# Scratch memory laid out anew, and VectorE's row sums of the feed-forward moved ahead of weight lows

## The chip, the cores and the metric

One NeuronCore of a Trainium2 chip runs the whole program. The metric is the device time of one execution in microseconds (us). Engines are named as in the profile: PE is TensorE's matmuls and PEld its weight loads, DVE is VectorE, ACT ScalarE, POOL GpSimd, SP the engine that issues the loads from HBM.

## What is computed

Four transformer layers over 512 tokens of width 1024, in fp32: two layers of a first stack (differential attention beside a gated linear recurrence, then a feed-forward part and a gate), two of a second (pooling mixer beside sparse attention, then a feed-forward part). The change touches the feed-forward parts, whose hidden width is 4096:

```python
h = h + jnp.square(jax.nn.relu(hm @ w_mlp_in[l])) @ w_mlp_out[l]      # layers 0 and 1
f = jnp.square(jax.nn.relu(h @ w_ff1[l])) @ w_ff2[l]                  # layers 2 and 3
x = x + rms_norm_2(f, g_post_ffn[l])
```

## The kernel before

**Products.** Activations lie transposed, 128 features on the partitions and 512 tokens along them. A fp32 product is made of three reduced-precision passes: each operand is split in a high part (a rounded copy, made by ScalarE) and a low part (value minus high part, made by VectorE), and TensorE adds high·high, high·low and low·high (`three_passes`, L472). Weights come in chunks of 1 MB (128 x 2048 values) in two raw buffers `wr`; `split_high` (L406) writes `wh`, `split_low` (L412) writes `wl`. SP loads chunk c once the low of chunk c - 2 is made (`load_chunk`, L375), since the raw buffer is then free.

**The feed-forward part** is done in four blocks of 1024 hidden features. A block has four input chunks (c0 to c0 + 3; each gives two tiles of hidden features in PSUM) and four output chunks. The first three blocks of every layer, twelve in all, are "fast": their output products are done by a seven-product scheme for 2 x 2 blocks, which needs sums and differences of quarters of the hidden tiles and of the weights. Blocks are counted from j = 0.

**VectorE in a fast block** (`fast_block_dve`) has for each input chunk i = 0 to 3, with p counting the pairs of tiles:
- `rectify` (L703): drains the even tile from PSUM, times the root of the mean square `rb`;
- `even_low` (L809, L810): its low part (128 x 256), and a first difference of quarters;
- `rectify` of the odd tile;
- for i < 2 the `split_low` (L412) of input chunk c0 + i + 2, not in block 0 of layers 2 and 3, where it was made earlier; for i = 2 four `form_low` (L781, 128 x 512 each) for the first output chunk;
- `other_sums` (L818, L819, L821), three sums of 128 x 256;
- for i = 3 one more `form_low`;
- `odd_low` (L828), 128 x 512;
- `sums_low` (L835, L838): the low of the first difference, 128 x 256, and of the three sums, 128 x 768, which go to the tile `rounded`.

**ScalarE** (`fast_block_act`) squares each tile (L789, L790), copies the high of the first difference (L796) between the two tiles, then `split_high` or four `form_high` (L769), then the high of the three sums (L802), which waits for L821. It works in the order it is given, and so does every engine.

**GpSimd** (`fast_block_pool`) forms four sums of 128 x 512 of the raw quarters of each output chunk (`sum_weights`, L752, L754, L756, L757) as soon as it is loaded. The second output chunk's load waits for the low of input chunk c0 + 3. Between them `carry` (L945) adds partial results to the output rows.

**TensorE** goes through the four input chunks (24 matmuls a tile) and straight on to the first output chunk (`fast_products`). There its first product needs L809 of pair 3 after three of four parts, and the four next products take their last part at the end, which needs L838 of pair 3. A tile's bank is free after its `rectify`.

**Layers 2 and 3** add the output to rows `branch(k)` in the scratch tile `arena`, which GpSimd zeroes with two memsets (L2070) before the first fast block; VectorE waits for them (`zeroed`) ahead of its first `rectify`. The first addition to these rows is `add_quarter` (L937), after the first output products.

**Memory.** Each partition holds, in this order: `gh`, `gl`, `hh`, `hl` (16 KB each), `arena` (15376 values, with `rounded` laid over the same place), `x`, `wr`, `wh`, `wl` (16 KB each), then small tiles.

Of the kernel before, what the change touches and what calls it, by code (L numbers as in the profile page):

```python
# [29 lines left out]
F32R = mybir.dt.float32r  # L30
# [6 lines left out]
P = 128  # L37
D = 1024
S = 512
# [8 lines left out]
BC = D // CW  # L48
FAST = FB - 1
HALF = S // 2  # L50
PAIRS = KT // 2
# [87 lines left out]
def build(nc, weights, params_a, params_b, gains, gates, embed, constants, positions, xt, out):  # L139

    with ExitStack() as ctx:
        def sb(name, shape, dtype=F32):
            return ctx.enter_context(nc.sbuf_tensor(name, shape, dtype))


        tiles = {name: sb(name, [P, KT, S], F32R) for name in ("gh", "gl", "hh", "hl")}
        with nc.sbuf_tensor("rounded", [P, ARENA], F32R) as rounded:
            pass
        arena = sb("arena", [P, ARENA])
        rest = dict(  # L150
            x=sb("x", [P, KT, S]), wr=sb("wr", [P, 2, CHUNK]), wh=sb("wh", [P, 2, CHUNK], F32R), wl=sb("wl", [P, 2, CHUNK], F32R),
            cst=sb("cst", [P, C_N]), par=sb("par", [P, max(AP_N, BP_N)]), rb=sb("rb", [P, S]), sq=sb("sq", [P, 2, S]),
            tmp=sb("tmp", [P, 4, S]), small=sb("small", [P, 256]), extra=sb("extra", [P, 7 * HALF + 2 * S]), rounded=rounded, arena=arena,
            ps=ctx.enter_context(nc.psum_tensor("ps", [P, 8, S], F32)))
        memories = [Memory(tiles["gh"], tiles["gl"], tiles["hh"], tiles["hl"], **rest),
                    Memory(tiles["hh"], tiles["hl"], tiles["gh"], tiles["gl"], **rest)]

        sets = [semaphores(nc, ctx, f"set{n}_", SET) for n in range(2)]
        shared = dict(zip(SHARED.split(), semaphores(nc, ctx, "shared", len(SHARED.split()))))
        stages = []  # L160
        for n in range(2 * DEPTH):
            stages.append(Stage(n, stages[-1] if stages else None, memories[n % 2], sets[n % 2], shared))
        for stage, following in zip(stages, stages[1:]):
            stage.following = following
        programs = []
        for n, stage in enumerate(stages):
            if n < DEPTH:
                programs.append(first_stack_layer(stage, n, weights, params_a, gains, gates, embed, constants, xt,
                                                  positions[0:P, :], positions[P:2 * P, :]))
            else:  # L170
                programs.append(second_stack_layer(stage, n - DEPTH, weights, params_b, gains, positions[P:2 * P, :], out))

        with nc.Block() as block:
            @block.sync
            def _(sp):
                for program in programs:
                    program["sp"](sp)

            @block.gpsimd
            def _(pool):  # L180
                for program in programs:
                    program["pool"](pool)

            @block.scalar
            def _(act):
                for program in programs:
                    program["act"](act)

            @block.vector
            def _(dve):  # L190
                for program in programs:
                    program["dve"](dve)

            @block.tensor
            def _(pe):
                for program in programs:
                    program["pe"](pe)
        used = [sem.num for sem in sets[0] + sets[1] + list(shared.values())]
        clear(nc, range(min(used), max(used) + 1))
# [138 lines left out]
ARENA = 15376  # L338
# [361 lines left out]
def rectify(dve, mem, sem, tile, k, per=once, bank=None):  # L700

    dve.wait_ge(sem["product"], tile + 1 + per(4 * BC))
    dve.scalar_tensor_tensor(out=mem.tmp[:, k % 2, :], in0=mem.ps[:, tile % 4 if bank is None else bank, :], scalar=0.0, in1=mem.rb[:, :],  # L703
                             op0=ALU.max, op1=ALU.mult).then_inc(sem["drained"], 1)
# [123 lines left out]
    dve.tensor_tensor(mem.hl[:, k, :], mem.tmp[:, 3, :], mem.hh[:, k, :].bitcast(F32), ALU.subtract).then_inc(sem["hidden_low"], 1)  # L828


def sums_low(dve, mem, sem, p):

    q = p % PAIRS
    dve.wait_ge(sem["sums_high"], 2 * p + 1)
    dve.tensor_tensor(mem.hl[:, 2 * q, HALF:S], mem.tmp[:, 2, 0:HALF], mem.hh[:, 2 * q, HALF:S].bitcast(F32), ALU.subtract)  # L835
    dve.wait_ge(sem["sums_high"], 2 * p + 2)
    dve.wait_ge(sem["hidden_sums"], 4 * p + 3)
    dve.tensor_tensor(mem.tl[:, q, :], mem.sums, mem.th[:, q, :].bitcast(F32), ALU.subtract).then_inc(sem["hidden_sums"], 1)  # L838
# [133 lines left out]
def fast_block_dve(dve, mem, sem, c0, j, tile_of, split_ahead, bank, target):  # L972

    for i in range(BC):
        p = PAIRS * j + i
        rectify(dve, mem, sem, tile_of[c0 + i], 2 * i, bank=bank(tile_of[c0 + i]))
        even_low(dve, mem, sem, p)
        rectify(dve, mem, sem, tile_of[c0 + i] + 1, 2 * i + 1, bank=bank(tile_of[c0 + i] + 1))
        if i < 2 and split_ahead:
            split_low(dve, mem, sem, c0 + i + 2)  # L980
        if i == 2:
            form_low(dve, mem, sem, c0 + BC, range(4))
        other_sums(dve, mem, sem, p)
        if i == 3:
            form_low(dve, mem, sem, c0 + BC, (4,))
        odd_low(dve, mem, sem, p)
        sums_low(dve, mem, sem, p)
    for oc in range(BC):
        g, c = BC * j + oc, c0 + BC + oc
        rows = target(2 * oc), target(2 * oc + 1)  # L990
        ahead = oc + 1 < BC
        if oc == 0:
            form_low(dve, mem, sem, c, (5, 6))
        first_partial(dve, mem, sem, g)
        if oc:
            form_low(dve, mem, sem, c, (6,))
        add_quarter(dve, mem, sem, g, "t", 3, rows[0][:, HALF:S])
        add_quarter(dve, mem, sem, g, "v", 4, rows[1][:, HALF:S])
        if not ahead:
            split_low(dve, mem, sem, c + 1)  # L1000
        second_partial(dve, mem, sem, g)
        if ahead:
            form_low(dve, mem, sem, c + 1, (0, 1))
        add_quarter(dve, mem, sem, g, "x", 6, rows[0][:, 0:HALF])
        if ahead:
            form_low(dve, mem, sem, c + 1, (2,))
        add_quarter(dve, mem, sem, g, "v", 7, rows[1][:, 0:HALF])
        if ahead:
            form_low(dve, mem, sem, c + 1, (3, 4, 5))
        else:  # L1010
            split_low(dve, mem, sem, c + 2)
# [901 lines left out]
def second_stack_layer(stage, layer, weights, params, gains, positions, out):  # L1913
# [301 lines left out]
    def program_dve(dve):  # L2215
# [261 lines left out]
                    split_low(dve, following.mem, following.sem, 2)  # L2477

        for j in range(FAST):
            if j == 0:  # L2480
                dve.wait_ge(sem["zeroed"], 2)
            fast_block_dve(dve, mem, sem, B_FF + 2 * BC * j, j, B_TILE, j > 0, b_bank, branch)
        c0 = B_CHUNKS - 2 * BC
        mlp_first(c0, FB - 1)
# [381 lines left out]
```

## Time and profile before

| what | us |
| --- | --- |
| median of 3 runs | 2491.5 |
| lowest and highest | 2491.39, 2491.71 |
| the profiled execution, its own time | 2496.87 |
| its span, first to last instruction | 2495.1 |
| mean granted TensorE clock | 0.985 |

The profile is of one execution, which took 5.4 us more than the median; times in the trace count from its first instruction. A timeline line gives start, duration, engine, line of the kernel, operation, output and inputs with their shapes, and in brackets how long the engine was idle before and what ended it. "x3" joins three like instructions. Lines of the kernel are those of the helper that issues the instruction.

### The profile page before, as it was taken

To read this page: it belongs to the slowest core of one execution; us is meant where nothing else is said; L and a number is where in the kernel's file an instruction comes from. 1 tells how busy PE (TensorE), PEld (TensorE's weight loads), DVE (VectorE), ACT (ScalarE), POOL (GpSimd) and SP (SyncE) were. 2 spreads that over 40 slices of the span, in tenths; PEclk is the share of its full clock that TensorE was granted. 3 is DMA by queue.
4 is the path that set the end of the run, shared out by engine and by line. 5 is a ranking of instruction groups with operands and counts; after the bars stand their busy time and mean duration, and the time that the engine had idled before them with its cause. 6 is when DMAs were issued, how large, how long until landed. Compare 5 with 4: busy or idle time off the path is not lost.

```text
span 2495.1 us, 34122 instructions
## 1 busy us (share of the span) xinstructions
PE 2395.5 (96%) x13186; PEld 1984.8 (80%) x13186; DVE 1737.2 (70%) x2881; ACT 1062.2 (43%) x1739; POOL 796.8 (32%) x606
## 2 busy tenths in 40 slices
PE   8999999999999999999999998999999999899997
PEld 6876888988787788898876876988886777788886
DVE  6786777845778577784569857786657966777753
ACT  4554434434355443443432453444343245434431
POOL 2002344501200243450247522352312832254412
PEclk9999999999999999999999999999999999899999
DMA  4211123132231212323222120322321211132231
GB/s 155 97 65 68 68 101 119 68 118 85 100 103 59 72 68 101 119 76 111 85 89 85 55 86 34 108 79 102 119 102 56 85 51 69 51 119 98 72 119 51
DMA packets 33230, 216.23 MB, mean 87 GB/s; under 512 B 4144, under 2 KB 4400, under 8 KB 8112
## 3 DMA queue, kind: packets, MB, share of 16 engines
q1 hardware_dynamic: 33072, 214.08, 24.3%
q8 instruction: 105, 1.72, 0.3%
q14 instruction: 53, 0.43, 0.1%
HBM read 211.97 MB, written 2.10 MB: 86 GB/s over the span
## 4 chain that ended last, share of the span: by engine, by line
PE 54%; DVE 14%; issue 13%; POOL 11%; ACT 5%; DMA 3%; SPq 0%; POOLq 0%; ACTq 0%; DVEq 0%
PE ps L472 47%; DVE wl L412 4%; DMA wr<-in_weights 3%; POOL arena L752 2%; ACT wh L406 2%; DVE wl L781 2%; POOL arena L754 2%; POOL arena L945 2%; POOL arena L757 1%; POOL arena L756 1%; POOL x L945 1%; DVE tmp L703 1%; PE ps L2622 1%; PE ps L2577 1%; DVE gl L694 1%
## 5 line engine op out<-in xcount | busy, mean ns | idle before, releaser
L472 PE MATMUL ps<-gh,wh 128*128 128x512 f32 (+2 forms) x1480 | 555.1, 375 | 33.9 <-DVE gl L694 10.3
L472 PE MATMUL ps<-hh,wh 128*128 128x512 f32 (+2 forms) x1448 | 540.6, 373 | 24.7 <-DVE hl L809 9.5
L472 PE MATMUL ps<-gl,wh 128*128 128x512 f32 (+2 forms) x1480 | 544.3, 368 | 0.0
L472 PE MATMUL ps<-gh,wl 128*128 128x512 f32 (+2 forms) x1480 | 543.9, 368 | 0.0
L472 PE MATMUL ps<-hh,wl 128*128 128x512 f32 (+2 forms) x1448 | 530.5, 366 | 0.0
L472 PE MATMUL ps<-hl,wh 128*128 128x512 f32 (+2 forms) x1448 | 530.4, 366 | 0.0
L412 DVE TENSOR_TENSOR wl<-wr,wh 128x2048 fp32r<-128x2048 f32 x120 | 278.5, 2321 | 197.1 <-ACT wh L406 194.9
L472 PEld LDWEIGHTS ps<-gh,wh 128*128 128x128 f32 (+1 forms) x1480 | 281.1, 190 | 99.7 <-issue 18.3
L406 ACT ACTIVATE wh<-wr 128x2048 fp32r<-128x2048 f32 x136 | 259.5, 1909 | 211.4 <-PE ps L472 125.8
L472 PEld LDWEIGHTS ps<-hh,wh 128*128 128x128 f32 (+1 forms) x1448 | 274.1, 189 | 87.2 <-issue 21.3
L472 PEld LDWEIGHTS ps<-gh,wl 128*128 128x128 f32 (+1 forms) x1480 | 281.1, 190 | 50.8
L472 PEld LDWEIGHTS ps<-gl,wh 128*128 128x128 f32 (+1 forms) x1480 | 280.7, 190 | 48.7 <-issue 1.4
L472 PEld LDWEIGHTS ps<-hh,wl 128*128 128x128 f32 (+1 forms) x1448 | 274.5, 190 | 48.9
L472 PEld LDWEIGHTS ps<-hl,wh 128*128 128x128 f32 (+1 forms) x1448 | 274.0, 189 | 47.3 <-issue 1.4
L472 PE MATMUL ps<-rounded,wh 128*128 128x256 f32 x1152 | 212.8, 283 | 4.6 <-DVE rounded L838 3.3
L781 DVE TENSOR_TENSOR wl<-arena,wh 128x512 fp32r<-128x512 f32 x192 | 179.4, 960 | 10.3 <-ACT wh L769 10.3
L769 ACT ACTIVATE wh<-arena 128x512 fp32r<-128x512 f32 x192 | 112.6, 625 | 171.0 <-POOL arena L754 86.3
L472 PEld LDWEIGHTS ps<-rounded,wh 128*128 128x128 f32 x1152 | 177.9, 191 | 7.1 <-DVE rounded L838 4.9
L472 PE MATMUL ps<-rounded,wl 128*128 128x256 f32 x576 | 162.3, 282 | 0.0
L703 DVE SCALAR_TENSOR_TENSOR tmp<-ps,rb 128x512 f32<-128x512 f32 x128 | 87.6, 686 | 99.1 <-PE ps L472 81.0
L781 DVE TENSOR_TENSOR wl<-wr,wh 128x512 fp32r<-128x512 f32 x144 | 142.0, 994 | 20.9 <-ACT wh L769 20.9
L752 POOL TENSOR_TENSOR arena<-wr 128x512 f32<-128x512 f32 x48 | 74.1, 1544 | 235.8 <-DMA wr<-in_weights 235.8
(303 smaller groups left out, 3703.7 us busy)
## 6 DMA issues: line engine op xcount, KB each, us to landing
wr<-in_weights SPq DMA_DIRECT2D x195, 1024.0 KB, 4.7
out_yt<-x SPq DMA_DIRECT2D x8, 256.0 KB, 2.0
x<-in_xt SPq DMA_DIRECT2D x3, 512.0 KB, 8.9
wr<-in_weights SPq DMA_DIRECT2D x2, 512.0 KB, 5.8
arena<-in_gates SPq DMA_DIRECT2D x2, 512.0 KB, 8.0
arena<-in_embed SPq DMA_DIRECT2D x2, 512.0 KB, 5.6
par<-in_params_b SPq DMA_DIRECT2D x2, 274.0 KB, 2.8
x<-in_xt SPq DMA_DIRECT2D x2, 256.0 KB, 4.6
```

Of the source, the lines that this page charges most:

```text
L406: act.activation(sem.high_part(c), mem.wr[:, sem.buffer(c), :], ACT.Copy).then_inc(sem["high"], 1)
L412: dve.tensor_tensor(sem.low_part(c), mem.wr[:, sem.buffer(c), :], sem.high_part(c).bitcast(F32), ALU.subtract)\
L472: done = pe.matmul(out, stationary, moving, start=(first and n == 0), stop=(last and n == 2), skip_group_check=True)
L694: dve.scalar_tensor_tensor(out=mem.gl[:, k, :], in0=mem.x[:, k, :], scalar=gains[:, k:k + 1], in1=mem.gh[:, k, :].bitcast(F32), op0=ALU.mu ...
L703: dve.scalar_tensor_tensor(out=mem.tmp[:, k % 2, :], in0=mem.ps[:, tile % 4 if bank is None else bank, :], scalar=0.0, in1=mem.rb[:, :], o ...
L752: pool.tensor_tensor(sums[:, 0, :], raw[:, 3, :], raw[:, 2, :], ALU.add).then_inc(sem["weight_sums"], 1)
L754: pool.tensor_tensor(sums[:, 1, :], sums[:, 0, :], raw[:, 0, :], ALU.subtract).then_inc(sem["weight_sums"], 1)
L756: pool.tensor_tensor(sums[:, 2, :], raw[:, 1, :], sums[:, 1, :], ALU.subtract).then_inc(sem["weight_sums"], 1)
L757: pool.tensor_tensor(sums[:, 3, :], raw[:, 0, :], raw[:, 3, :], ALU.subtract).then_inc(sem["weight_sums"], 1)
L769: act.activation(sem.form(c, f)[0], weight_form(mem, sem, c, f), ACT.Copy) .then_inc(sem["high" if f == FORMS - 1 else "form_high"], 1)
L781: done = dve.tensor_tensor(low, weight_form(mem, sem, c, f), high.bitcast(F32), ALU.subtract)
L945: last = pool.tensor_tensor(target[row][:, part], target[row][:, part], u[:, n, :], ALU.add)
```

## The change

The tile `arena` and the tile `rounded` over it are placed behind `wl` instead of before `x`; `x`, `wr`, `wh` and `wl` move down by the arena's size, all other tiles stay. In `fast_block_dve` L835 goes directly behind the odd `rectify`; `other_sums`, the fifth `form_low` and `odd_low` follow; the weights' lows (`split_low`, or four `form_low`) come next, and L838 last. The wait for `zeroed` moves from before block 0 to its first addition. ScalarE, GpSimd, TensorE and SP keep their programs.

```diff
         tiles = {name: sb(name, [P, KT, S], F32R) for name in ("gh", "gl", "hh", "hl")}
-        with nc.sbuf_tensor("rounded", [P, ARENA], F32R) as rounded:
-            pass
-        arena = sb("arena", [P, ARENA])
         rest = dict(
             x=..., wr=..., wh=..., wl=...,
+            rounded=overlaid("rounded", [P, ARENA], F32R), arena=sb("arena", [P, ARENA]),
             cst=..., par=..., rb=..., sq=...,
...
-def sums_low(dve, mem, sem, p):
+def first_sum_low(dve, mem, sem, p):
     q = p % PAIRS
     dve.wait_ge(sem["sums_high"], 2 * p + 1)
     dve.tensor_tensor(mem.hl[:, 2 * q, HALF:S], ...)                      # L835
+def other_sums_low(dve, mem, sem, p):
+    q = p % PAIRS
     dve.wait_ge(sem["sums_high"], 2 * p + 2)
     dve.wait_ge(sem["hidden_sums"], 4 * p + 3)
     dve.tensor_tensor(mem.tl[:, q, :], mem.sums, ...)                     # L838
...
         rectify(dve, mem, sem, tile_of[c0 + i] + 1, 2 * i + 1, bank=bank(tile_of[c0 + i] + 1))
+        first_sum_low(dve, mem, sem, p)
+        other_sums(dve, mem, sem, p)
+        if i == 3:
+            form_low(dve, mem, sem, c0 + BC, (4,))
+        odd_low(dve, mem, sem, p)
         if i < 2 and split_ahead:
             split_low(dve, mem, sem, c0 + i + 2)
         if i == 2:
             form_low(dve, mem, sem, c0 + BC, range(4))
-        other_sums(dve, mem, sem, p)
-        if i == 3:
-            form_low(dve, mem, sem, c0 + BC, (4,))
-        odd_low(dve, mem, sem, p)
-        sums_low(dve, mem, sem, p)
+        other_sums_low(dve, mem, sem, p)
...
         if oc == 0:
             form_low(dve, mem, sem, c, (5, 6))
+            if sem.stage.second:
+                dve.wait_ge(sem["zeroed"], 2)
         first_partial(dve, mem, sem, g)
...
         for j in range(FAST):
-            if j == 0:
-                dve.wait_ge(sem["zeroed"], 2)
             fast_block_dve(dve, mem, sem, B_FF + 2 * BC * j, j, B_TILE, j > 0, b_bank, branch)
```

## Rows read from the trace of the kernel before

**Rows 1.** The profile page, part 1: busy time, share of the span, instructions.

```profile
PE 2395.5 (96%) x13186; PEld 1984.8 (80%) x13186; DVE 1737.2 (70%) x2881; ACT 1062.2 (43%) x1739; POOL 796.8 (32%) x606
```

**Rows 2.** TensorE's waits: for whom, us in total, times, longest us.

```profile
PE ps L472 <- DVE tmp L703: 15.9, 2, 8.0
...
PE ps L472 <- DVE gl L809: 9.9, 6, 4.2
PE ps L472 <- DVE hl L809: 9.5, 6, 4.0
...
PE ps L472 <- DVE rounded L838: 3.3, 8, 0.5
```

**Rows 3.** Timeline of TensorE: start us, us, operation, [idle before, releaser].

```profile
286.86 0.58 PE L472 MATMUL ps<-hh,wh 128*128 128x256 f32 x1 [3.98 <-DVE hl L809]
...
375.16 0.39 PE L472 MATMUL ps<-hh,wh 128*128 128x256 f32 x1 [0.59 <-DVE hl L809]
...
380.34 0.50 PE L472 MATMUL ps<-rounded,wh 128*128 128x256 f32 x2 [0.48 <-DVE rounded L838]
...
909.61 0.39 PE L472 MATMUL ps<-gh,wh 128*128 128x256 f32 x1 [4.23 <-DVE gl L809]
...
1542.74 0.77 PE L472 MATMUL ps<-gh,wh 128*128 128x512 f32 x1 [7.97 <-DVE tmp L703]
...
1560.81 0.39 PE L472 MATMUL ps<-hh,wh 128*128 128x256 f32 x1 [3.14 <-DVE hl L809]
...
2171.38 0.38 PE L472 MATMUL ps<-gh,wh 128*128 128x256 f32 x1 [2.94 <-DVE gl L809]
```

**Rows 4.** Windows after three waits: bounds, us, PE, PEld, DVE, ACT, POOL, granted clock, DMA, GB/s.

```profile
285.20:292.10 6.90, 5.24 (x24) 5.25 (x25) 5.20 (x12) 5.56 (x11) 0.00 (x0) 0.51 0.00 1
909.90:913.30 3.40, 3.40 (x18) 3.40 (x18) 2.70 (x6) 3.08 (x6) 0.00 (x0) 0.50 0.00 0
...
1561.80:1565.20 3.40, 3.40 (x18) 3.40 (x17) 2.82 (x7) 3.29 (x6) 0.00 (x0) 0.50 0.00 0
```

**Rows 5.** Timeline of VectorE and GpSimd, first layer, second fast block.

```profile
343.70 2.29 DVE L412 TENSOR_TENSOR wl<-wr,wh 128x2048 fp32r<-128x2048 f32 x1 [3.03 <-ACT wh L406]
345.92 0.42 DVE L818 TENSOR_TENSOR extra<-tmp 128x256 f32<-128x256 f32 x1
...
348.80 0.68 DVE L703 SCALAR_TENSOR_TENSOR tmp<-ps,rb 128x512 f32<-128x512 f32 x1
...
350.99 1.44 POOL L752 TENSOR_TENSOR arena<-wr 128x512 f32<-128x512 f32 x1 [19.69 <-DMA wr<-in_weights]
351.19 0.69 DVE L703 SCALAR_TENSOR_TENSOR tmp<-ps,rb 128x512 f32<-128x512 f32 x1
...
354.91 2.44 DVE L412 TENSOR_TENSOR wl<-wr,wh 128x2048 fp32r<-128x2048 f32 x1 [3.03 <-ACT wh L406]
...
362.31 1.32 POOL L752 TENSOR_TENSOR arena<-wr 128x512 f32<-128x512 f32 x1 [3.79 <-DMA wr<-in_weights]
...
363.83 1.51 DVE L810 TENSOR_TENSOR tmp<-tmp 128x256 f32<-128x256 f32 x1
...
367.69 0.69 DVE L781 TENSOR_TENSOR wl<-wr,wh 128x512 fp32r<-128x512 f32 x1 [1.75 <-ACT wh L769]
...
372.99 0.68 DVE L703 SCALAR_TENSOR_TENSOR tmp<-ps,rb 128x512 f32<-128x512 f32 x1
```

**Rows 6.** Timeline of GpSimd and VectorE, third layer, first fast block.

```profile
1525.20 3.56 POOL L2070 MEMSET arena<- 128x3072 f32 x2
...
1529.84 0.69 DVE L703 SCALAR_TENSOR_TENSOR tmp<-ps,rb 128x512 f32<-128x512 f32 x1 [2.25 <-ACT rb L683]
...
1553.34 0.69 DVE L781 TENSOR_TENSOR wl<-wr,wh 128x512 fp32r<-128x512 f32 x1 [1.74 <-ACT wh L769]
```

**Rows 7.** TensorE's groups by form: x count | busy us, mean ns.

```profile
L472 PE MATMUL ps<-rounded,wh 128*128 128x256 f32 x1152 | 212.8, 283 | 4.6 <-DVE rounded L838 3.3 <-DVE wl L781 1.3
...
L472 PE MATMUL ps<-hh,wh 128*128 128x256 f32 x384 | 109.6, 286 | 9.7 <-DVE hl L809 9.5
```

More of the change, by code:

```diff
@@ L143, in sb, with overlaid @@
             return ctx.enter_context(nc.sbuf_tensor(name, shape, dtype))
+        def overlaid(name, shape, dtype):
+            with nc.sbuf_tensor(name, shape, dtype) as place:
+                return place
         tiles = {name: sb(name, [P, KT, S], F32R) for name in ("gh", "gl", "hh", "hl")}
-        with nc.sbuf_tensor("rounded", [P, ARENA], F32R) as rounded:
-            pass
-        arena = sb("arena", [P, ARENA])
         rest = dict(
             x=sb("x", [P, KT, S]), wr=sb("wr", [P, 2, CHUNK]), wh=sb("wh", [P, 2, CHUNK], F32R), wl=sb("wl", [P, 2, CHUNK], F32R),
+            rounded=overlaid("rounded", [P, ARENA], F32R), arena=sb("arena", [P, ARENA]),
             cst=sb("cst", [P, C_N]), par=sb("par", [P, max(AP_N, BP_N)]), rb=sb("rb", [P, S]), sq=sb("sq", [P, 2, S]),
-            tmp=sb("tmp", [P, 4, S]), small=sb("small", [P, 256]), extra=sb("extra", [P, 7 * HALF + 2 * S]), rounded=rounded, arena=arena,
+            tmp=sb("tmp", [P, 4, S]), small=sb("small", [P, 256]), extra=sb("extra", [P, 7 * HALF + 2 * S]),
             ps=ctx.enter_context(nc.psum_tensor("ps", [P, 8, S], F32)))
```

## The prediction

> **What bounds the kernel now.** I read the page first: TensorE is busy for 2395.5 us of a span of 2495.1 us, VectorE for 1737.2 us [rows 1]. So only what TensorE waits for, and the clock it is granted, can be won or lost here. Next TensorE's waits: in the fast blocks it waits 9.9 + 9.5 us for L809 (12 times, once a block), 3.3 us for L838 (8 times) and 15.9 us for a `rectify` (twice, one line) [rows 2]. The timeline of TensorE says where: 3.98 and 4.23 us in block 0 of layers 0 and 1, 3.14 and 2.94 us in block 0 of layers 2 and 3, and what is left of the 19.4 us in the eight later blocks, as the 0.59 us at 375.16 with 0.48 us for L838 behind it [rows 3]. Last, the windows after the long ones: the granted clock is 0.51 from 285.2 to 292.1 and 0.50 from 909.9 to 913.3 and from 1561.8 to 1565.2, the lower level of 1.2 GHz [rows 4]. Half of the work time at half clock is lost: 5.24/2 = 2.6 us, 1.7 us and 1.7 us. These losses follow the waits directly.
>
> So VectorE is late when TensorE turns from input to output products, and the question is whether the new order makes L809 and L838 of the last pair earlier.
>
> **Where VectorE loses its time.** In a later block of layer 0, VectorE stands idle 3.03 us before each `split_low` (343.70, 354.91) and 1.75 us before the first L781 (367.69), for ScalarE's copies [rows 5]. The sums moved ahead have their inputs then. Filled fully, that is 3.03 + 3.03 + 1.75 = 7.8 us of idle per block. What of it arrives at L809 of pair 3 has two obstacles, both in the same rows.
>
> First, the tiles: the odd `rectify` of i = 1 at 351.19 runs when its product is there; the even one at 348.80 could come 2 us earlier, this one by 0.2 us only.
>
> Second, collisions with GpSimd. L818 alone takes 0.42 us (345.92); L810 at 363.83 takes 1.51 us while GpSimd's weight sums run [rows 5]. Its end, 365.34, lies just behind the end of one GpSimd sum (1.3 to 1.4 us each), so I count one VectorE instruction of two SBUF inputs per GpSimd sum, short or long; a `rectify` (PSUM input, 0.69 us beside L752) goes free. Four sums last about 5.6 us. The old order met them with long instructions: the `split_low` of 2048 values at 354.91 took 2.44 us, hardly more than the 2.29 us at 343.70 [rows 5]. The new order meets them with the short ones.
>
> Of this the Trainium skill (SBUF — State Buffer, Who interferes with whom) says that such a VectorE instruction and a GpSimd instruction that reads SBUF exclude each other, and that "Issue order, not op shape, decides who blocks." The rows at 354.91 and 363.83 agree that the second waits. Read strictly it would let a VectorE instruction that comes between two sums win; that is the first rival below.
>
> **The schedule by hand, later blocks (eight).** Units: L703 to the even low's input 1.7 us; a 256-wide operation 0.34 us after another, 512-wide 0.6, L838 0.9, `split_low` 2.2.
> - i = 0: behind `split_low` (343.70 + 2.2) only L838 is left, where five more stood. Even `rectify` of i = 1 at 346.8 instead of 348.80; the odd one at 351.0 instead of 351.19.
> - i = 1: GpSimd's sums run from 350.99 to about 356.6. L835 and L818 to L821 meet them and end at 352.3, 354.0, 355.4 and 356.8; L828 at 357.4; `split_low` 357.4 to 359.7, 2.3 us later than before; L838 to 360.6. Even `rectify` of i = 2 at 360.5, about 0.7 us earlier than before.
> - The second output chunk's load waits for that low. Before, 362.31 less the low's end at 357.35 is 4.96 us; so GpSimd's next sums begin at 364.65, not 362.31.
> - i = 2: L809 and L810 are free of them now (before, L810 paid 1.1), but L819, L821, L828 and the first L781 meet them at about 1.4 to 1.8 each, the other three L781 follow at 0.6, L838 at 0.9: even `rectify` of i = 3 at 373.7, against 372.99 [rows 5]. I take 0.66 us later.
> - L809 of pair 3 is 0.66 us later: TensorE waits 0.59 + 0.66 = 1.25 us.
> - i = 3: L835 is out of the way of L838, so L838 comes 0.66 - 0.34 = 0.3 us later, while TensorE arrives 0.66 us later: its wait of 0.48 falls to about 0.1 us.
> The same counting on the old order gives 373.1 for the row's 372.99. **Cost 0.3 us a block, 8 x 0.3 = +2.5 us.** Bounds: both waits gone, -(0.6 + 0.45), or one more collision of 1.4 us.
>
> **Block 0 of layers 0 and 1.** Here the tiles are ready long before VectorE comes (3.98 us late at the end), so the first obstacle is absent and 2 us are won at i = 0. At i = 1 the sums L818 and L819 are through before GpSimd begins; L821, L828 and part of `split_low` are hit; 1.4 us are left. At i = 2 five short operations are hit instead of two. L809 comes 0.85 us earlier. If the clock falls and rises there when it did before [rows 4], part of the work that comes earlier goes at half speed: I count 0.6 us each. **2 x -0.6 = -1.2 us.** Bounds: nothing, or the whole wait and the low clock, 3.98 + 2.6 and 4.23 + 1.7 us.
>
> **Block 0 of layers 2 and 3.** No `split_low` inside, and GpSimd is done with its sums by i = 2. At i = 0 VectorE has collisions already (until 1540) and the third `rectify` waits for ScalarE's L802 behind L821; L835 moved ahead fits in the idle 0.7 us before L818, so the wait of 7.97 us stays. At i = 2 the idle 1.74 us before L781 [rows 6] is filled by L818 to L828 (three times 0.34 and 0.6, from 0.7 us after the `rectify`): L809 of pair 3 comes 1.3 us earlier, and the waits of 3.14 and 2.94 us [rows 3] become 1.8 and 1.6. **2 x -1.3 = -2.6 us.** The low clock of 3.4 us behind it costs 1.7 us; whether it still comes after the shorter wait no row shows; I take half, **-1.7 us**, bounds 0 and -3.4.
>
> **The `zeroed` wait.** The memsets end at 1528.76 and the first `rectify` starts at 1529.84, released by ScalarE's `rb` [rows 6]: the old wait costs nothing. At its new place, some 38 us later, it costs nothing either. Behind it on VectorE is the first addition, for which GpSimd's `carry` waits; both are far off. In layers 0 and 1 no wait is added.
>
> **The placement.** No instruction is added or changed, only addresses. The nearest rows: matmuls that read `rounded` (now moved) take 283 ns, those that read `hh` (not moved) 286 ns [rows 7]. I take 0. Bounds by their difference of 3 ns over 1728 matmuls (1152 with `wh`, half as many with `wl`): ±5 us. The Trainium skill (SBUF — State Buffer, SBUF: two separate sides) names no cost of an address either, only of shared ports; by it the sum would be the same.
>
> **Sum:** +2.5 - 1.2 - 2.6 - 1.7 = -3.0 us. On the profiled execution's own 2496.87 us this is 2493.9 us; it lies 5.4 us over the median, so on the median of 2491.5 us the forecast is **2488.5 us**. A measurement of this kernel can tell about 0.2%, 5 us, from no change.
>
> **Rivals.**
> 1. *VectorE wins the collisions.* If its short instructions are through before GpSimd's sums, or the next load comes later, L809 and L838 of the last pair are in time: the waits of 19.4 + 3.3 us go but for 3.4 us in block 0 of layers 2 and 3, and with them low clock of 2.6 + 1.7 + 1.7 + 1.7 us. 2491.5 - 27 = 2464.5 us in full; half of it, 2478, is likelier. For: the idle 7.8 us a block. Against: GpSimd's sums start at 350.99, just where the idle time of i = 1 begins. Chance of more than 5 us gained: 0.34.
> 2. *Slower: weight lows too late.* The low of c0 + 3 comes 2.3 us later, and GpSimd's sums shift with it onto i = 2. If one more instruction per block meets a sum, L809 of pair 3 comes 1.4 us later in ten blocks that split ahead: 2488.5 + 14 = 2502.5 us. It decides from six blocks on (8 us turns -3 into +5). In block 0 of layers 0 and 1 the low has besides only about a microsecond to spare before its chunk is wanted. For: GpSimd's start is tied to the late low. Against: L809 and L810 get free. Chance of more than 5 us lost: 0.18.
> 3. *The placement matters,* by up to 5 us either way; held in both chances.
> 4. *Nothing happens:* VectorE's idle time only moves, 2491.5 us. With my forecast this is the case within 0.2%: 0.48.
>
> **Range.** Half of rival 1 below, 2478, and about half of rival 2 above, 2497; this leaves out some 2 in 10.
>
> **What would show it.** VectorE idle before `split_low` under 1 us at i = 0 in later blocks; L818 to L821 of i = 1 at 1.4 us each instead of 0.42; GpSimd's second group of sums 2.3 us later; waits for L809 of 1.2 us in later blocks, about 3.2 us in block 0 of layers 0 and 1, 1.8 us in block 0 of layers 2 and 3, still 7.97 us for the third `rectify`. Wrong if the waits for L809 in later blocks vanish or pass 2 us, if the short operations stay at 0.42, or if matmul durations of `rounded` move by more than 1%.

## The result and the profile after

| what | before | after |
| --- | --- | --- |
| median of 4 runs, us | 2491.61 | 2471.23 |
| lowest and highest | 2491.39, 2492.46 | 2469.79, 2472.72 |
| the profiled execution, its own time | 2496.87 | 2469.79 |
| its span | 2495.1 | 2468.0 |
| mean granted TensorE clock | 0.985 | 0.986 |

The ratio of the times is 0.9918, with an interval of 0.99 to 0.9935: 20.4 us faster, where 3 us were forecast, and below the range of 2478 to 2497. (The two profiled executions lie 27.1 us apart, since the one of the kernel before took some 5 us more than its median.) In the page's part 1, TensorE is busy for 29.4 us less and VectorE for 57.4 us more than in [rows 1], each with as many instructions as before:

```profile
PE 2366.1 (96%) x13186; PEld 1998.3 (81%) x13186; DVE 1794.6 (73%) x2881; ACT 1058.8 (43%) x1739; POOL 787.5 (32%) x606
```

TensorE's waits (for whom, us in total, times, longest us), against [rows 2]. L811 is the L809 of before, L705 the L703, L474 the L472:

```profile
PE ps L474 <- DVE tmp L705: 16.3, 2, 8.1
PE ps L474 <- DVE hl L811: 14.0, 6, 4.1
PE ps L474 <- DVE gl L811: 13.9, 6, 3.4
```

The kernel waits longer for VectorE, not less: 27.9 us for the low of the last even tile instead of 19.4. Only the wait for `rounded` has gone (3.3 us before). What got shorter is TensorE's own work, and that stands in its groups by form (x count | busy us, mean ns). First before, then after:

```profile
L472 PE MATMUL ps<-gl,wh 128*128 128x512 f32 x1088 | 433.5, 398 | 0.0
```

```profile
L474 PE MATMUL ps<-gl,wh 128*128 128x512 f32 x1088 | 426.3, 392 | 0.0
...
L474 PE MATMUL ps<-rounded,wh 128*128 128x256 f32 x1152 | 219.3, 287 | 0.0
```

In `ps<-gl,wh` the first name behind the arrow is the tile that streams through TensorE, the second the tile that the weights are loaded from. A matmul of 512 columns shows 6 ns less; one of 256 columns with `rounded` shows 4 ns more than in [rows 7]. These durations overlap, since matmuls are pipelined, so the cadence is better read from start to start. Two stretches of TensorE's timeline before, the first in a linear layer, the second in a fast block:

```profile
520.53 0.39 PE L472 MATMUL ps<-gl,wh 128*128 128x512 f32 x1
...
521.70 0.40 PE L472 MATMUL ps<-gh,wh 128*128 128x512 f32 x1
```

```profile
391.11 0.28 PE L472 MATMUL ps<-hl,wh 128*128 128x256 f32 x1
...
391.68 0.28 PE L472 MATMUL ps<-hh,wh 128*128 128x256 f32 x1
```

and after:

```profile
520.36 0.39 PE L474 MATMUL ps<-gl,wh 128*128 128x512 f32 x1
...
521.72 0.39 PE L474 MATMUL ps<-gl,wh 128*128 128x512 f32 x1
...
905.00 0.28 PE L474 MATMUL ps<-gh,wh 128*128 128x256 f32 x1
...
905.96 0.28 PE L474 MATMUL ps<-gh,wl 128*128 128x256 f32 x1
```

Before, five matmuls of 512 columns take 1.17 us (0.234 each); after, six take 1.36 us (0.227 each). With 256 columns five took 0.57 us (0.114 each) and now eight take 0.96 us (0.120 each). Both kernels run these stretches at full clock. (Loads from HBM run beside some of them and not beside others; the sums over whole traces, further below, say the same.) So in these stretches the long matmuls became 3% quicker and the short ones 5% slower, in a change that touches no matmul. Over the whole traces, at full clock, the means are 0.233 and 0.227 us for the long ones, 0.116 and 0.120 us for the short ones.

**The new order in the profile.** VectorE and GpSimd in the second fast block of the first layer, against [rows 5]:

```profile
337.45 2.29 DVE L414 TENSOR_TENSOR wl<-wr,wh 128x2048 fp32r<-128x2048 f32 x1 [0.63 <-ACT wh L408]
...
344.80 1.29 POOL L754 TENSOR_TENSOR arena<-wr 128x512 f32<-128x512 f32 x1 [19.45 <-DMA wr<-in_weights]
...
346.31 1.51 DVE L820 TENSOR_TENSOR extra<-tmp 128x256 f32<-128x256 f32 x1
...
347.74 1.51 DVE L821 TENSOR_TENSOR extra<-tmp 128x256 f32<-128x256 f32 x1
...
349.18 1.51 DVE L823 TENSOR_TENSOR extra<-tmp,extra 128x256 f32<-128x256 f32 x1
...
351.21 2.28 DVE L414 TENSOR_TENSOR wl<-wr,wh 128x2048 fp32r<-128x2048 f32 x1
...
358.42 1.52 POOL L754 TENSOR_TENSOR arena<-wr 128x512 f32<-128x512 f32 x1 [8.02 <-DMA wr<-in_weights]
```

The reader sees the filled idle time (0.63 us before the first `split_low`, was 3.03), the three sums at 1.51 us each beside GpSimd's sums (they follow each other every 1.44 us), and the second group of GpSimd's sums, which now starts 13.6 us after the first instead of 11.3.

TensorE's timeline at the waits, against [rows 3]: block 0 and a later block of layer 0, block 0 of layer 1, then layer 2 with the third `rectify` and block 0, and block 0 of layer 3:

```profile
281.64 0.39 PE L474 MATMUL ps<-hh,wh 128*128 128x256 f32 x1 [4.12 <-DVE hl L811]
...
456.06 0.39 PE L474 MATMUL ps<-hh,wh 128*128 128x256 f32 x1 [2.13 <-DVE hl L811]
...
897.46 0.58 PE L474 MATMUL ps<-gh,wh 128*128 128x256 f32 x1 [3.37 <-DVE gl L811]
...
1525.82 0.76 PE L474 MATMUL ps<-gh,wh 128*128 128x512 f32 x1 [8.13 <-DVE tmp L705]
1542.42 0.39 PE L474 MATMUL ps<-hh,wh 128*128 128x256 f32 x1 [1.50 <-DVE hl L811]
...
2144.65 0.39 PE L474 MATMUL ps<-gh,wh 128*128 128x256 f32 x1 [2.21 <-DVE gl L811]
```

The eight later blocks wait 1.98 to 2.20 us each, where they waited 0.47 to 1.02. Windows of 3.2 us right behind four of the waits, the first of them behind the wait of 2.08 us at 369.48 (bounds, us, TensorE busy and its matmuls, granted clock, DMA share, GB/s), against [rows 4]:

```profile
369.78:372.98 3.20, 3.20 (x29) 1.00 0.00 0
456.36:459.56 3.20, 3.20 (x19) 0.56 0.03 5
...
1542.72:1545.92 3.20, 3.20 (x29) 1.00 0.00 0
...
2144.95:2148.15 3.20, 3.20 (x29) 1.00 0.00 0
```

Behind the waits of block 0 in layers 2 and 3 the low clock is gone. In exchange it came behind five of the eight later waits (456.06, 985.07, 1715.46, 2231.09 and 2319.01), where the kernel before had none.

### The profile page after: what moved, and what is told of

The parts are those of the page before. It is cut to its first block, busy times and chain, and to the rows that moved or that the text cites. A ratio compares the mean times of both kernels' runs of the same rounds, so it can differ in the third digit from the quotient of the medians.

```text
span 2468.0 us, 34122 instructions
## 1 busy us (share of the span) xinstructions
PE 2366.1 (96%) x13186; PEld 1998.3 (81%) x13186; DVE 1794.6 (73%) x2881; ACT 1058.8 (43%) x1739; POOL 787.5 (32%) x606
## 4 chain that ended last, share of the span: by engine, by line
PE 70%; DVE 21%; ACT 4%; issue 2%; POOL 1%; DMA 0%; SPq 0%; POOLq 0%; DVEq 0%; ACTq 0%
PE ps L474 63%; DVE wl L414 2%; DVE wl L783 2%; DVE tmp L705 1%; DVE extra L823 1%; ACT tmp L791 1%; DVE arena L2317 1%; DVE rounded L845 1%; DVE small L2312 1%; DVE extra L820 1%; PE ps L2630 1%; DVE extra L821 1%; PE ps L2585 1%; DVE gl L696 1%; PE ps L2663 1%
## 5 line engine op out<-in xcount | busy, mean ns | idle before, releaser
L474 PE MATMUL ps<-gh,wh 128*128 128x512 f32 (+2 forms) x1480 | 550.5, 372 | 35.8 <-DVE gl L811 13.9
L474 PE MATMUL ps<-hh,wh 128*128 128x512 f32 (+2 forms) x1448 | 534.8, 369 | 27.6 <-DVE hl L811 14.0
L474 PE MATMUL ps<-gl,wh 128*128 128x512 f32 (+2 forms) x1480 | 539.4, 364 | 0.0
L474 PE MATMUL ps<-gh,wl 128*128 128x512 f32 (+2 forms) x1480 | 539.3, 364 | 0.0
L474 PE MATMUL ps<-hh,wl 128*128 128x512 f32 (+2 forms) x1448 | 525.2, 363 | 0.0
L474 PE MATMUL ps<-hl,wh 128*128 128x512 f32 (+2 forms) x1448 | 525.1, 363 | 0.0
L474 PEld LDWEIGHTS ps<-gh,wh 128*128 128x128 f32 (+1 forms) x1480 | 282.2, 191 | 93.5 <-issue 18.9
L474 PEld LDWEIGHTS ps<-hh,wh 128*128 128x128 f32 (+1 forms) x1448 | 275.0, 190 | 81.7 <-issue 20.8
L474 PEld LDWEIGHTS ps<-gh,wl 128*128 128x128 f32 (+1 forms) x1480 | 282.0, 191 | 44.8
L474 PEld LDWEIGHTS ps<-gl,wh 128*128 128x128 f32 (+1 forms) x1480 | 282.5, 191 | 42.8 <-issue 1.4
L474 PEld LDWEIGHTS ps<-hh,wl 128*128 128x128 f32 (+1 forms) x1448 | 274.8, 190 | 42.9
L474 PEld LDWEIGHTS ps<-hl,wh 128*128 128x128 f32 (+1 forms) x1448 | 275.1, 190 | 41.5 <-issue 1.4
L474 PE MATMUL ps<-rounded,wh 128*128 128x256 f32 x1152 | 219.3, 287 | 0.0
L783 DVE TENSOR_TENSOR wl<-arena,wh 128x512 fp32r<-128x512 f32 x192 | 189.2, 1010 | 2.5 <-ACT wh L771 2.5
L474 PEld LDWEIGHTS ps<-rounded,wh 128*128 128x128 f32 x1152 | 183.5, 196 | 0.5
L474 PE MATMUL ps<-rounded,wl 128*128 128x256 f32 x576 | 165.4, 287 | 0.0
L705 DVE SCALAR_TENSOR_TENSOR tmp<-ps,rb 128x512 f32<-128x512 f32 x128 | 87.5, 685 | 105.6 <-PE ps L474 87.8
L791 ACT ACTIVATE tmp<-tmp 128x512 f32<-128x512 f32 x96 | 60.6, 632 | 220.9 <-DVE tmp L705 220.9
```

What stands on the lines that cost most here:

```text
L474: done = pe.matmul(out, stationary, moving, start=(first and n == 0), stop=(last and n == 2), skip_group_check=True)
L783: done = dve.tensor_tensor(low, weight_form(mem, sem, c, f), high.bitcast(F32), ALU.subtract)
L791: act.activation(value, source, ACT.Square).then_inc(sem["hidden_high"], 1)
```

## The experiments

The theory after the result: placement gives the gain, by the start of the weight tiles `wh` and `wl`, and the order gives what was forecast. Its rivals: the gain is the order's; or it is the region of the memory in which the tiles lie; or it is the alignment of other tiles. All kernels compute the whole reference. In the tables "us" is the run's median, "before" the median of the kernel before on the same chip at the same time, and then come their ratio and its interval. "wh at" is its first byte modulo 256.

**The parts alone.** e1 has only the new placement, e2 only the new order, e3 only the moved wait, and e4 the new placement with 64 bytes ahead of `x`:

```diff
 # e4, on top of e1
         tiles = {...}
+        sb("pad", [P, 16])
         rest = dict(
             x=..., wr=..., wh=..., wl=...,
```

> Theory P (the placement makes TensorE's 512-column matmuls quicker, and that is the gain): the 512-column products go on at about 0.228 us each instead of 0.2335, those of 256 columns at 0.1225 instead of 0.117, and the time is about 2471 us or a little less. Theory O (the new order of VectorE is the gain): the time stays within 3 us of 2491.5 us, and the matmuls go on as before. My prediction had 0 for this part, with bounds of 5 us.

> The new order alone, with the memory and the wait for zeroed rows as before. Theory P, and my prediction: within 5 us of 2491.5, most likely 2488 us; waits for the even low of the last pair 1.2 us in the later blocks, 1.8 us in block 0 of layers 2 and 3. Theory O: about 2471 us.

> Only the wait for zeroed rows moved. All theories: no difference, within 1 us of 2491.5, since the first rectify is released by the root of the mean square after the memsets end. If the wait had cost something: up to 1 us less in each of layers 2 and 3.

> Placement alone, but with 64 bytes put before x, so that x, wr, wh, wl, arena and all behind them lie 64 bytes further. In the kernel before x, wr, wh and wl began at 64 modulo 128 bytes, in the changed one at 0. If the alignment to 128 bytes is the cause: back to about 2491 us and 0.2335 us a matmul. If it is the region of memory: as placement alone, about 2471 us.

| run | us | before | ratio, interval | wh at |
| --- | --- | --- | --- | --- |
| e1 placement | 2472.19 | 2491.48 | 0.9922, 0.9905 to 0.9938 | 0 |
| e2 order | 2486.87 | 2491.48 | 0.9981, 0.9972 to 0.9991 | 64 |
| e3 wait | 2492.81 | 2491.48 | 1.0002, 0.9992 to 1.0011 | 64 |
| e4 placement and 64 bytes | 2492.68 | 2491.48 | 1.0006, 0.9997 to 1.0016 | 64 |

The placement gives 19.3 us by itself, the order 4.6 us, the moved wait nothing. 64 bytes take the placement's gain away whole, so it isn't the region. The same groups as above, e1 first, then e2:

```profile
L475 PE MATMUL ps<-gl,wh 128*128 128x512 f32 x1088 | 426.4, 392 | 0.0
...
L475 PE MATMUL ps<-rounded,wh 128*128 128x256 f32 x1152 | 219.0, 287 | 1.9 <-DVE rounded L841 1.9
```

```profile
L471 PE MATMUL ps<-gl,wh 128*128 128x512 f32 x1088 | 433.3, 398 | 0.0
...
L471 PE MATMUL ps<-rounded,wh 128*128 128x256 f32 x1152 | 210.6, 281 | 3.9 <-DVE wl L780 3.2
```

The quicker long matmuls and the slower short ones both come with the placement. The waits of e2 are the purest look at the order. TensorE's timeline in e2, block 0 and a later block of layer 0, and block 0 of layers 2 and 3:

```profile
285.41 0.58 PE L471 MATMUL ps<-hh,wh 128*128 128x256 f32 x1 [3.38 <-DVE hl L808]
...
373.32 0.38 PE L471 MATMUL ps<-hh,wh 128*128 128x256 f32 x1 [1.42 <-DVE hl L808]
...
1556.40 0.39 PE L471 MATMUL ps<-hh,wh 128*128 128x256 f32 x1 [1.95 <-DVE hl L808]
...
2162.35 0.56 PE L471 MATMUL ps<-gh,wh 128*128 128x256 f32 x1 [2.75 <-DVE gl L808]
```

**How far off, and which tile.** e5 and e6 shift tiles of the old layout, e7 to e9 put 64, 32 and 128 bytes between `wr` and `wh` of the new one, e10 and e11 put 512 and 2048 there. e12 is the old layout, with `arena` still before `x` and 4032 bytes behind it, by which `wh` starts at 163840:

```diff
 # e6 and e7 (64 bytes: 16 values); e8: 8, e9: 32, e10: 128, e11: 512, e15: 64 values
-            x=..., wr=sb("wr", [P, 2, CHUNK]), wh=sb("wh", [P, 2, CHUNK], F32R), wl=...,
+            x=..., wr=sb("wr", [P, 2, CHUNK]),
+            wh=(sb("pad", [P, 16]), sb("wh", [P, 2, CHUNK], F32R))[1], wl=...,
```

```diff
 # e5: [P, 16], e12: [P, 1008]
         arena = sb("arena", [P, ARENA])
+        sb("pad", [P, 16])
```

> The memory in the order of before (arena ahead of x), with 64 bytes put behind the arena, so that x, wr, wh and wl begin at 0 modulo 128 bytes. Theory L (the alignment to 128 bytes of the tiles behind the arena decides): about 2472 us and 0.2275 us a 512-column matmul. Theory R (the place of the tiles in memory decides, and the 64 bytes of the last run moved them out of it by chance): about 2491 us and 0.2335 us.

> The memory of before with 64 bytes put between wr and wh: x and wr stay at 64 modulo 128 bytes, wh and wl come to 0. If it is what TensorE loads as weights (wh and wl) that has to be aligned: about 2472 us, 0.2275 us a 512-column matmul. If it is x or wr: about 2491 us. If VectorE's or ScalarE's work is what changed: in between, with TensorE's matmuls as before.

> The new placement with 64 bytes put between wr and wh: x and wr at 0 modulo 128 bytes, wh, wl and arena at 64. If wh and wl decide: about 2491 us and 0.2335 us. If x and wr decide: about 2472 us.

> The new placement with 32 bytes put between wr and wh: wh, wl and arena at 32 modulo 128 bytes. If any place off 128 bytes costs the same: about 2491 us and 0.2335 us. If the cost grows as the place is less aligned: more than 2491 us. If only 64 modulo 128 is slow: about 2472 us.

> The new placement with 128 bytes between wr and wh, so that wh and wl begin at 98432 and 114816 bytes of a partition, 128 modulo 256. The run with 64 bytes put behind the old arena showed that 128 bytes of alignment are not enough. Theory G (a coarser alignment of wh and wl, of 256 bytes or more, is needed): about 2491 us, 0.233 us a matmul. Theory R (the region below 131072 bytes is what counts, and runs of 32 and 64 bytes were slow for a reason of their own): about 2472 us.

> As before, with 512 bytes, the length of the row of one weight load. Theory G with up to 512 bytes: about 2472 us, 0.2275 us a matmul. If the alignment must be coarser still: about 2491 us.

> As before, with 2048 bytes, the length of a moving row of 512 values. Theory G with up to 2048 bytes: about 2472 us. If slow, too, it must be coarser still, or the exact places of the changed kernel matter.

> The memory in the order of before, with 4032 bytes behind the arena, so that x, wr, wh and wl begin at 131072, 147456, 163840 and 180224 bytes, multiples of 16384 as in the changed kernel, but 65536 bytes higher. Theory G: about 2472 us, 0.2275 us a matmul. Theory R (region): about 2491 us, 0.2335 us.

| run | us | before | ratio, interval | wh at |
| --- | --- | --- | --- | --- |
| e5 | 2488.32 | 2490.49 | 0.999, 0.998 to 1.0 | 128 |
| e6 | 2491.73 | 2490.49 | 1.0003, 0.9992 to 1.0013 | 128 |
| e7 | 2492.55 | 2490.49 | 1.0011, 1.0 to 1.0021 | 64 |
| e8 | 2492.97 | 2490.49 | 1.001, 1.0 to 1.0021 | 32 |
| e9 | 2490.7 | 2491.76 | 0.9994, 0.9984 to 1.0005 | 128 |
| e10 | 2471.48 | 2491.76 | 0.9919, 0.9899 to 0.9938 | 0 |
| e11 | 2471.58 | 2491.76 | 0.992, 0.9901 to 0.994 | 0 |
| e12 | 2473.08 | 2491.76 | 0.9925, 0.9905 to 0.9944 | 0 |

32, 64 and 128 bytes cost about the same, and the old region with aligned weights is as good as the new one. The first theory, that a start at a multiple of 128 bytes is enough, had 2472 us for e5 and e6 and is refuted by them and by e9. In e5 and e6 `wh` starts at the same byte and `x` and `wr` 64 bytes apart; the 3 us between their medians, of one interval's size, settle nothing. TensorE's group `gl,wh` in e9 and in e10:

```profile
L476 PE MATMUL ps<-gl,wh 128*128 128x512 f32 x1088 | 431.3, 396 | 0.0
```

```profile
L476 PE MATMUL ps<-gl,wh 128*128 128x512 f32 x1088 | 426.6, 392 | 0.0
```

Next, which tile. e13 moves `x`, `wr` and `arena` off by 64 bytes and keeps `wh` and `wl` on multiples of 512; e14 is off in `wh` alone, with all others on multiples of 256; e15 puts `wh` and `wl` at 256 modulo 512:

```diff
 # e13
-            x=sb("x", ...), wr=..., wh=sb("wh", ...), wl=sb("wl", ...),
+            x=(sb("pad0", [P, 16]), sb("x", ...))[1], wr=...,
+            wh=(sb("pad1", [P, 112]), sb("wh", ...))[1], wl=(sb("wl", ...), sb("pad2", [P, 16]))[0],
 # e14
+            x=sb("x", ...), wr=...,
+            wh=(sb("pad0", [P, 16]), sb("wh", ...))[1],
+            wl=(sb("pad1", [P, 112]), sb("wl", ...))[1],
```

> The new placement, with x, wr and arena 64 bytes off 128, and wh and wl at multiples of 512 bytes. If wh and wl alone decide: about 2472 us, 0.228 us a 512-column matmul. If the raw buffers, the residual or the arena matter too: up to 2491 us, with VectorE, ScalarE or GpSimd instructions longer.

> wh 64 bytes off, wl at a multiple of 512 bytes. Two of three passes load their weights from wh. If each weight load counts for itself: about two thirds of the loss, 2485 us, and the passes with wl quick, those with wh slow. If the slowest decides: 2491 us; if only wl counts: 2472 us.

> wh and wl at 256 modulo 512 bytes; 128 was slow and 512 quick. Either 2491 us (the row of 512 bytes of a weight load has to begin at its own multiple) or 2472 us (256 bytes are enough). I expect the first, six to four.

| run | us | before | ratio, interval | wh at |
| --- | --- | --- | --- | --- |
| e13 | 2470.48 | 2493.04 | 0.9914, 0.9898 to 0.9931 | 0 |
| e14 | 2491.09 | 2493.04 | 0.9994, 0.9984 to 1.0004 | 64 |
| e15 | 2472.64 | 2493.04 | 0.9919, 0.9903 to 0.9936 | 0 |

The gain hangs on `wh`: with `x`, `wr` and `arena` off it stays, with `wh` alone off it is gone. A start at a multiple of 256 bytes is enough, where six to four had been expected for the opposite. Of the three passes two load their weights from `wh`, one from `wl`; a kernel with `wl` alone off was not run. The passes on the aligned `wl` of e14 are no quicker than those on `wh` (0.234 and 0.232 us from start to start for 512 columns), as they would be if each weight load counted for itself.

The traces hold more than the times. Mean time from one matmul's start to the next at full clock, in us, over the whole trace, for weights in `wh` and `wl`. The last two columns are the matmuls of 256 columns, with activations streaming and with `rounded` streaming; `rounded` lies where `arena` does:

| start past a multiple of 256 bytes | runs | 512 columns | 256, activations | 256, `rounded` |
| --- | --- | --- | --- | --- |
| 0 | changed, e1, e10, e11, e12, e15 | 0.227 | 0.120 | 0.120 |
| 0, `rounded` at 64 | e13 | 0.227 | 0.120 | 0.118 |
| 32, `rounded` too | e8 | 0.233 | 0.118 | 0.119 |
| 64 | before, e2, e3 | 0.233 | 0.114 to 0.116 | 0.114 to 0.116 |
| 64, `rounded` too | e4, e7 | 0.233 | 0.115 | 0.118 |
| 128 (e9: `rounded` too) | e5, e6, e9 | 0.233 | 0.119 | 0.119 |

So the short matmuls are clearly quicker at 64 bytes only, and there the place of the tile that streams counts as well.

**Both cadences at once.** Long matmuls want weights on a multiple of 256 bytes, and short ones are quicker with weights 64 bytes off one. e16 is the changed kernel with `wh` and `wl` 128 values wider in each half, and with the quartered weights of the fast blocks 64 bytes further inside them; whole chunks stay on a multiple of 256. e17 is the same layout with VectorE's old order. e18 is the same layout with the new order, but in input chunk i = 1 `split_low` keeps its old place ahead of the sums:

```diff
 # e16
+        self.shifted = tuple(w[:, :, FORM_SHIFT:FORM_SHIFT + CHUNK] for w in (wh, wl))   # FORM_SHIFT = 16
+        self.wh, self.wl = wh[:, :, 0:CHUNK], wl[:, :, 0:CHUNK]
...
+            wh=sb("wh", [P, 2, CHUNK + 128], F32R), wl=sb("wl", [P, 2, CHUNK + 128], F32R),
...
-        return self.stage.mem.wh[:, home, part], self.stage.mem.wl[:, home, part]
+        return tuple(w[:, home, part] for w in self.stage.mem.shifted)
 # e18, on top of e16
-        first_sum_low(dve, mem, sem, p)
+        if i != 1:
+            first_sum_low(dve, mem, sem, p)
+        elif split_ahead:
+            split_low(dve, mem, sem, c0 + i + 2)
         other_sums(dve, mem, sem, p)
...
-        if i < 2 and split_ahead:
+        if i == 0 and split_ahead:
             split_low(dve, mem, sem, c0 + i + 2)
+        if i == 1:
+            first_sum_low(dve, mem, sem, p)
```

> The changed kernel, with wh and wl widened by 512 bytes a half, and the seven forms of the fast chunks written and read 64 bytes further, so that the input chunks stay at multiples of 512 bytes and only the forms are off. If the 256-column matmuls are slower for their weights' alignment: 0.1146 us each instead of 0.120, up to 4032 x 0.0054 = 22 us less, so 2450 to 2465 us, as far as VectorE and GpSimd keep up. If something else holds the fast blocks at a period of about 86.1 us: 2471 us, and the matmuls stay at 0.120.

> The layout of the last run (input chunks at multiples of 512 bytes, fast forms 64 bytes further), with VectorE's old order in the input chunks. If the new order is worth what it was worth alone (4.6 us): 2469 us. If it is worth nothing where TensorE comes earlier to the last pair: 2464 us. If VectorE's low of the last pair holds the block: waits of about 1.5 us for it in the later blocks and 0.5 us for the low of the sums behind it.

> The same layout and the new order, except in input chunk 1, where the weights' low stays ahead of the row sums: there the low comes 2.3 us earlier, GpSimd's second group of sums with it, and it is the long instruction again that meets the first group. Worked out by the same counting as in the prediction: the even low of the last pair 1.1 us earlier in each of the eight later blocks and 0.8 us in block 0 of layers 0 and 1, so 2464 - 8 = 2456 us. If collisions with GpSimd are not what holds VectorE: no difference from 2464 us.

| run | us | before | ratio, interval |
| --- | --- | --- | --- |
| e16 changed kernel, shifted quarters | 2464.3 | 2493.04 | 0.9891, 0.9875 to 0.9908 |
| e17 with VectorE's old order | 2466.87 | 2494.03 | 0.9893, 0.9876 to 0.9909 |
| e18 with the mixed order | 2452.07 | 2494.03 | 0.9828, 0.9811 to 0.9844 |

In e16 both groups are quick:

```profile
L478 PE MATMUL ps<-gl,wh 128*128 128x512 f32 x1088 | 426.2, 392 | 0.0
...
L478 PE MATMUL ps<-rounded,wh 128*128 128x256 f32 x1152 | 212.4, 283 | 2.7 <-DVE wl L787 2.1
```

The fast output phase of a later block, from its first to its last matmul of 256 columns with the waits between, lasts 40.4 to 41.4 us before, 42.3 to 42.5 in e1, 41.3 to 41.7 in e17 and 40.5 to 41.1 in e18. e16 and e17 differ by less than their intervals: once the weights are aligned, the new order as a whole is worth nothing that can be told. The trace of e18 suggests why. VectorE, GpSimd and TensorE in its second block:

```profile
345.20 1.29 POOL L758 TENSOR_TENSOR arena<-wr 128x512 f32<-128x512 f32 x1 [19.39 <-DMA wr<-in_weights]
...
348.79 2.60 DVE L418 TENSOR_TENSOR wl<-wr,wh 128x2048 fp32r<-128x2048 f32 x1 [3.02 <-ACT wh L412]
...
351.31 1.51 DVE L824 TENSOR_TENSOR extra<-tmp 128x256 f32<-128x256 f32 x1
352.75 0.41 DVE L825 TENSOR_TENSOR extra<-tmp 128x256 f32<-128x256 f32 x1
...
356.31 1.29 POOL L758 TENSOR_TENSOR arena<-wr 128x512 f32<-128x512 f32 x1 [3.77 <-DMA wr<-in_weights]
...
368.83 0.39 PE L478 MATMUL ps<-hh,wh 128*128 128x256 f32 x1 [0.97 <-DVE hl L815]
```

The long `split_low` takes the collisions with GpSimd's sums (2.60 us here, 2.51 to 3.02 over the ten blocks, 2.29 alone; GpSimd's fourth sum takes 3.34 us beside it, 1.46 in the changed kernel), one short sum of this input chunk pays 1.51 us instead of three, and the second group of GpSimd's sums starts 11.1 us after the first instead of 13.6. The later waits fall to 0.90 to 1.30 us, the ones of block 0 in layers 2 and 3 stay short (2.24 and 1.95 us), and of the twelve windows behind the waits only two are at low clock, those of block 0 in layers 0 and 1. The waits in total:

```profile
PE ps L478 <- DVE hl L815: 10.0, 6, 3.4
PE ps L478 <- DVE gl L815: 9.8, 6, 3.4
```

e18 beats both kernels: 2494.03 - 2452.07 = 42.0 us below the kernel before, where the change has 20.4 us. Its median lies 12.2 us below that of e16 (of another session), from which it differs in input chunk 1 alone; how much of this is the cheaper collisions and how much GpSimd's earlier second group, no run takes apart. Against e17 it is 14.8 us: by the profiles the wait in block 0 is 1.4 to 1.6 us shorter in each of the four layers, the low clocks of layers 2 and 3 are gone, the eight later waits are shorter by 0.3 us each, and of 3.4 us for `rounded` none is left. These parts make some 15 us, but the two profiled executions lie only 9.4 us apart (e18's took 5.5 us more than its median), and the difference is not accounted for.

## Why the prediction was wrong

**The step that failed is the placement.** The prediction says "No instruction is added or changed, only addresses ... I take 0", with bounds of ±5 us from the 3 ns between matmuls that read `rounded` and those that read `hh` [rows 7]. Those rows compare the tile that streams through TensorE. In both rows the weights come from the same `wh`, which lay at 159808, 64 bytes past a multiple of 256. So these rows could not bound what moves with `wh`, and the multiplier was as wrong as the unit: 1728 matmuls instead of the 10464 that load weights from `wh` or `wl`. The trace of the kernel before did hold rows that could. In the last layer some weights are split into `gh` and `gl`, which start on multiples of 16384 bytes, and the same `hl` streams over weights from either place, with 512 columns (kernel before):

```profile
L472 PE MATMUL ps<-hl,wh 128*128 128x512 f32 x1056 | 419.0, 397 | 0.0
...
L472 PE MATMUL ps<-hl,gh 128*128 128x512 f32 x48 | 18.7, 390 | 0.0
```

7 ns apart, and in the changed kernel 390 and 389 ns: an estimate from this difference over 6432 matmuls gives a bound of 45 us, not 5. Measured (e1): -19.3 us. Its parts come from adding up, over a whole trace, the times from one matmul's start to the next less the idle time; e3 stands for the old placement, since its profiled execution (2488.81 us) lies nearer to the medians than that of before. The 6432 matmuls of 512 columns on `wh` or `wl` take 1535.0 us in e3 and 1497.5 in e1, -37.5 us; the 4800 of 256 columns, 4032 of them on `wh` or `wl`, take 575.5 and 591.7, +16.2 us; TensorE's idle time, in gaps over 0.15 us, is 78.0 and 81.3 us, +3.3 us, more of it for the even low and less elsewhere. That is -18.0 of the 18.4 us between the two executions (2488.81 and 2470.45). Rival 3 named the placement, with the size of the same wrong bound. That the time fell, as forecast, is luck: 19.3 of the 20.4 us come from the term taken at 0.

**The Trainium skill** (SBUF — State Buffer, SBUF: two separate sides) was cited as naming no cost of an address; e4 and e1, 20.5 us apart by 64 bytes, show one, and the measurement decides.

**The later blocks** were right. Forecast: waits for L809 of 1.25 us and for L838 of about 0.1; e2 shows 1.21 to 1.42 us and no wait for L838, and a block of layer 0 (375.16 to 461.42 before, 373.32 to 459.98 in e2) 0.4 us longer, where 0.3 was forecast; over the four layers it is 0.2 us in the mean. In the changed kernel the same 0.6 to 0.7 us come on top of e1's 1.36 to 1.60 us, which gives the 1.98 to 2.20 us measured. There lies what the sum had not: the cost of an added wait depends on how long the wait is already. The later waits of e1 and those of e2 leave the clock at full; the longer ones of the changed kernel were followed by low clock five times in eight, which costs some 1.2 us each time (the fast output phase lasts 43.9 to 44.1 us with it and 42.7 to 42.8 without).

**Block 0 of layers 0 and 1** was right: 0.85 us of each wait was to go, and 0.60 and 0.87 us went in e2 (3.98 to 3.38, 4.23 to 3.36).

**Block 0 of layers 2 and 3** was right in layer 2 and missed in layer 3: forecast waits of 1.8 and 1.6 us, measured in e2 1.95 and 2.75 us, so that 1.19 and 0.19 us went where 1.3 each were to go. Why layer 3 kept its wait is open. Of the low clock behind them half was taken, and in e2 it is gone in one of the two (clock 1.00 from 1556.70 to 1559.90, 0.50 from 2162.65 to 2165.85). The third `rectify` kept its wait (8.01 us in e2, 8.13 in the changed kernel), as forecast.

**The `zeroed` wait** costs nothing (e3), as forecast.

**The order's sum**, -3.0 us (-3.1 with 8 x 0.3 = 2.4), stands against -4.6 us in e2 (interval -7.0 to -2.2): right within what can be measured. Rival 2, that the weight lows come too late, has its mechanism (the second sums 2.3 us later, and e18's gain from taking that part back) but not its price, since L809 and L810 ran free as the schedule by hand had it. Rival 1 did not happen; its number was reached by another way. Of the signs of being wrong two fired. The matmul durations of `rounded` moved by 1.4% (283 to 287 ns); this sign alone watched the placement. And the waits for L809 in later blocks pass 2 us in six of eight cases (up to 2.20 us); e2, without the placement, has 1.42 us at most, so this too comes from the placement's longer waits under the order's.

**On the new placement the order is worth about nothing** (2471.23 against e1's 2472.19), though it had been worth 4.6 us. By the traces: block 0 wins 0.86 and 1.62 us in layers 0 and 1 and 2.59 and 1.42 us in layers 2 and 3, and two low clocks; the later blocks lose 0.65 us eight times and five low clocks of 1.2 us, and gain 1.9 us of waits for `rounded`. The two sides are about equal.

**What stays open:** why TensorE goes on more slowly with weights that start off a multiple of 256 bytes when 512 columns stream through, and faster at 64 bytes when 256 do. Weight loads run beside matmuls (busy for 80% and 96% of the span [rows 1]), so one might look for it between the load and the streaming of the other operand; no run here takes these apart. The tiles that stream in matmuls of 512 columns (`gh`, `gl`, `hh`, `hl`) start on multiples of 16384 bytes in every run, so for these it is not shown whether the start of the weights counts by itself or against that of the streamed tile. Nor was it tried what small stationary tiles in `small` or inside `arena` lose.

## What to carry to other kernels

Before a layout is called free, look where the tiles that TensorE loads as weights start, and compare kernels that differ in this alone; a bound taken from rows that all share one address bounds nothing, and the same trace may hold rows with another. Start weights of matmuls of 512 columns at multiples of 256 bytes, and try 64 bytes off for those of 256. Let one long VectorE instruction meet a group of GpSimd's, not several short ones, and keep the short ones for idle time in which GpSimd is silent.

## What the runs showed of the hardware that was not expected

- The start of the weight tile sets TensorE's cadence. In fp32 passes of 512 columns it is 0.233 us in the mean at 32, 64 or 128 bytes past a multiple of 256, and 0.227 us on one (e1, e10 to e13, e15); for this kernel 2491 against 2472 us. With 256 columns it is the other way at 64 bytes, 0.114 to 0.116 against 0.120 us, and hardly at all at 32 and 128 (0.118 to 0.119). Both can be had in one kernel (e16: 0.227 and 0.115 us; its median is 6.9 us below the changed kernel's, of another session, and the intervals of the two ratios just overlap).
- Low clock behind a wait of TensorE is not settled by the wait's length. Behind the waits for L809 of up to 1.95 us none came, behind those of 2.75 us and more it always came, and between 1.98 and 2.30 us both are seen (2.08 us at 369.48: clock 1.00 behind it; 2.13 us at 456.06: 0.56).
- Beside GpSimd's sums a VectorE instruction of 256 values a partition takes 1.51 us instead of 0.42, one of 512 values 1.78 us instead of 0.68 (L830 at 360.14, changed kernel), and one of 2048 values 2.43 to 2.48 us in the kernel before and 2.51 to 3.02 us in e18 instead of 2.29: the price is per instruction and does not grow with its length.
